# The first keys, the block scores and a table's layout around the input projection of a two-layer decoder trunk

## The reference, cut to what matters

```python
h = rmsnorm(x, a_norm);  proj = h @ w_in
qa, kc, vc, ksl, vsl, kwn, vwn, ga, qb, kb, vb, fb = split(proj)
qa = rope(rmsnorm(heads(qa)));  ksl, kwn = rope(rmsnorm(...))     # "first keys": ksl, kwn
k_cmp = rope(rmsnorm(gelu(blocks(kc) @ w1) @ w2));  v_cmp = ...    # 15 compressed blocks
p_c = masked_softmax(qa @ k_cmp);  o_c = p_c @ v_cmp               # "block scores"
o_s, o_w = selected and window branches                            # 256 keys: all of them
o_a = gates * (o_c, o_s, o_w)
qb, kb = rmsnorm(qb), rmsnorm(kb);  cum = cumsum(log_sigmoid(fb))
o_b = masked_softmax(qb @ kb + cum_q - cum_k) @ vb                 # fox heads
x = x + concat(o_a, o_b) @ w_out
```

## Time and profile before

| | before |
|---|---|
| runs | 1252.96, 1253.08, 1251.99 us (median 1252.96) |
| profiled execution, its own time | 1252.75 us |
| its span | 1250.9 us |
| PE busy | 1233.9 us, 99% of the span |
| PE weight loads / DVE / ACT / POOL busy | 82% / 79% / 65% / 3% |
| mean granted TensorE clock | 0.996 of full |

### The profile page before, as it was taken

One profiled execution on the slowest core, in us unless ns is written; L12 is line 12 of the kernel. 1 busy time (PEld: TensorE's weight loads), 2 busy tenths in 40 slices (PEclk: granted clock), 3 DMA queues, 4 the chain that ended last, 5 costly groups with the idle time before them and its releaser, 6 DMA issues.

```text
span 1250.9 us, 16182 instructions
## 1 busy us (share of the span) xinstructions
PE 1233.9 (99%) x6016; PEld 1021.7 (82%) x6021; DVE 982.4 (79%) x966; ACT 817.2 (65%) x891; POOL 36.5 (3%) x42
## 2 busy tenths in 40 slices
PE   8999999999999999999999999999999999999998
PEld 6789888888889886888888888888888888888886
DVE  5878664544567558999889889889889889889896
ACT  7555454343376547777777777777777777777774
POOL 1000000000000001000000000000000000000200
PEclk9899999999999999999999999999999999999999
DMA  9631135544444345999999999999999999999992
GB/s 356 253 135 35 53 150 202 202 179 172 169 184 143 131 152 201 361 392 373 398 365 375 398 365 371 398 372 368 395 355 368 408 381 368 387 369 364 396 420 92
DMA packets 53000, 361.36 MB, mean 289 GB/s; under 512 B 6048, under 2 KB 6560, under 8 KB 10944
## 3 DMA queue, kind: packets, MB, share of 16 engines
q1 hardware_dynamic: 49872, 349.34, 72.4%
q0 software_dynamic: 3056, 11.02, 2.2%
HBM read 354.56 MB, written 5.77 MB: 288 GB/s over the span
## 4 chain that ended last, share of the span: by engine, by line
PE 94%; DVE 2%; DMA 1%; SPq 1%; issue 1%; ACT 0%; DVEq 0%
PE bank L561 28%; PE bank L559 28%; PE bank L560 28%; PE bank L1099 2%; DMA raw<-in_weights 1%; PE bank L770 1%; PE bank L800 1%; PE bank L958 1%; PE bank L782 1%; PE bank L569 1%; PE bank L1064 0%; PE bank L669 0%; PE bank L846 0%; PE bank L716 0%; PE bank L1056 0%
## 5 line engine op out<-in xcount | busy, mean ns | idle before, releaser
L2150 DVE TENSOR_TENSOR low<-raw,whi 128x2048 fp32r<-128x2048 f32 x260 | 595.1, 2291 | 72.0 <-ACT whi L1497 70.8
L1497 ACT CAST whi<-raw 128x2048 fp32r<-128x2048 f32 x260 | 497.3, 1913 | 120.8 <-PE bank L561 119.8
L559 PE MATMUL bank<-whi,hT_hi 128*128 128x512 f32 (+1 forms) x1104 | 431.4, 391 | 1.7 <-DVE low L1646 1.1
L561 PE MATMUL bank<-whi,hT_lo 128*128 128x512 f32 (+1 forms) x1104 | 430.5, 390 | 0.0
L560 PE MATMUL bank<-low,hT_hi 128*128 128x512 f32 (+1 forms) x1104 | 429.8, 389 | 0.0
L559 PEld LDWEIGHTS bank<-whi,hT_hi 128*128 128x128 f32 x1104 | 208.1, 188 | 46.0 <-DVE hT_lo L1581 1.5
L560 PEld LDWEIGHTS bank<-low,hT_hi 128*128 128x128 f32 x1104 | 207.8, 188 | 43.8
L561 PEld LDWEIGHTS bank<-whi,hT_lo 128*128 128x128 f32 x1104 | 207.7, 188 | 43.1
L1563 DVE TENSOR_TENSOR low<-raw,whi 128x2048 fp32r<-128x2048 f32 x67 | 153.0, 2288 | 48.3 <-ACT whi L1190 48.2
L559 PE MATMUL bank<-whi,h_hi 128*128 128x512 f32 x440 | 183.1, 416 | 0.0
L561 PE MATMUL bank<-whi,h_lo 128*128 128x512 f32 x440 | 174.5, 397 | 0.0
(11 more groups left out here) (313 smaller groups left out, 823.6 us busy)
## 6 DMA issues: line engine op xcount, KB each, us to landing
raw<-in_weights SPq DMA_DIRECT2D x327, 1024.0 KB, 5.9
sums<-ybuf POOLq DMA_DIRECT2D x7, 512.0 KB, 6.9
arena<-in_compress SPq DMA_DIRECT2D x1, 1088.0 KB, 15.4
x<-in_x SPq DMA_DIRECT2D x2, 512.0 KB, 5.2
raw<-in_weights SPq DMA_DIRECT2D x4, 256.0 KB, 5.4
raw<-in_weights SPq DMA_DIRECT2D x2, 512.0 KB, 8.1
tokens<-hng POOLq DMA_DIRECT2D x2, 512.0 KB, 3.5
out<-x SPq DMA_DIRECT2D x4, 256.0 KB, 3.0
```

The costliest lines, as they stand in the source:

```text
L559: mm(out_, a_hi, b_hi, start=start, stop=False)
L561: return mm(out_, a_lo, b_hi, start=False, stop=stop)
L1497: nc.scalar.copy(whi[:, u % SPLIT, :, :], raw[:, u % RAW, :, :]).then_inc(S["w_hi"], 1)
L2150: V.tensor_tensor(low[:, u % RAW, :, :], raw[:, u % RAW, :, :], whi[:, u % SPLIT, :, :].bitcast(F32), ALU.subtract).then_inc(S["w_lo"], 1)
```

## The change

Four things: the table `sml` gets 124 more columns (426 to 550), with most entries at other places; on ACT the squares of group 0 come behind the copies of its result, and PE waits ahead of group 2 for the squares, since both use banks 4 and 5; on DVE `split(5)` moves behind the first keys; on PE `block_scores` moves from the middle of group 5 to its end.

```diff
-R_QN, R_KN, R_FQ, R_FK, R_ON, R_GB, R_FB, R_EPS = 0, 64, 128, 129, 130, 132, 156, 164
-R_NORM = 166
+R_QN, R_KN, R_FQ, R_FK, R_ON, R_GB, R_FB, R_EPS = 0, 64, 128, 129, 256, 258, 282, 130
+R_NORM = 290
@@ PE, in_group
                 if cg >= 2:
                     pe.wait_ge(S["proj"], 2 * (cg - 1))
+                if cg == 2:
+                    pe.wait_ge(S["squares"], 2)
@@ PE
-            in_group(5, {2: later_queries, 4: block_scores})
+            in_group(5, {2: later_queries})
+            block_scores()
             pe.wait_ge(S["head_done"], 4)
@@ ACT
-                if cg == 0:
-                    head_squares(0, 0, 256)
...
                 if cg == 0:
+                    head_squares(0, 0, 256)
                     head_root(0, 8)
@@ DVE
             head_sums(4, 0)
-            split(5)
...
             head_roots(4, 0)
             link(head_scale(keys, 4, 0, R_KN, keys))
             rope(keys, tab, 4, four(rA, 4), four(rB, 4)).then_inc(S["head_done"], 1)
+            split(5)
             dve.wait_ge(S["sw_hi"], 2)
```

## The result

| | before | after |
|---|---|---|
| median of the runs taken together | 1253.02 us (4 runs) | 1245.76 us (4 runs: 1246.83, 1245.91, 1245.61, 1245.12) |
| profiled execution, its own time; its span | 1252.75; 1250.9 | 1246.83; 1245.0 |
| PE busy | 1233.9 us | 1226.1 us |
| mean granted clock | 0.996 | 0.996 |

The ratio is 0.9944 with a 95% interval of 0.9927 to 0.9961: faster by 7.3 us (4.9 to 9.1). The forecast was 1253.6 us in 1250.4 to 1257.0. PE's busy time alone fell by 7.8 us, and around the input projection the new kernel has one more wait above 1 us than the old one (two for one).

A forecast was written before the change was run, and what follows sets the result against it. PE was taken as the bound, in the chain for 94% of 1250.9 us; -1.34 - 1.7 + 2.5 + 1.3 = +0.8 us on 1252.75 gave 1253.6 us, range 1250.4 to 1257.0.

The forecast's parts named there:

- The longer table: 124 more columns in `sml` shift the tiles declared behind it: 0, with bounds of -2 and +2 us.
- Rival four: The tiles' new places pay, up to 2 us or more off the sum: 1249.5 to 1251; chance 0.04.
- The wait and the keys: Input projection: DVE's keys ahead of split(5) remove PE's wait before the 64 small products, -1.34 us.
- PE's wait for the squares: Ahead of group 2: the new wait does not bind, 0 us, bounds 0 and 0.3 us.
- The clock at the first place: Near 45 us: 3.4 us at half clock in place of 6.7, -1.7 us, bounds -3.4 and 0.
- rival one: Behind group 5 the clock stays low into the attention: slower, 1255.3 or 1257.0 us; chance 0.25.
- The block scores: Behind group 5: without the second unit as cover, the chain through ACT and DVE delays PE, +2.5 us.
- the term of the clock: Behind group 5: 38 thin products make the clock fall again, +1.3 us, bounds 0 and +4.7.
- The table load on ACT: Before the exponential behind group 5: 1.28 us by the trace, without the 1.38 us drain of the skill's rule.
- The sum of the moves: Input projection and behind group 5 together: -1.34 - 1.7 + 2.5 + 1.3 = +0.8 us.
- the 459 GB/s: Rate assumed while the first units load: the table's 63 KB more take 0.14 us, counted as 0.

The follow-up runs named there:

- t_table: The kernel before with the longer table alone, no engine's order moved: 1244.83 us, ratio 0.9947.
- b_table_keys: The changed kernel with the block scores put back between the two units of group 5: 1241.44 us, ratio 0.9907.
- a_short_table: The changed kernel with the short table put back, so the three moves alone: 1254.20 us, ratio 1.0015.
- r_all128: The changed kernel with 128 bytes of pad ahead of the first tile, moving all tiles together: 1246.09 us, ratio 0.9951.
- t_pad224: The kernel before, old table, with the pad ahead of the attention's area 224 bytes wider: 1245.52 us, ratio 0.9945.
- t_pad480: The kernel before, old table, with the pad ahead of the attention's area 480 bytes wider: 1243.71 us, ratio 0.9922.
- p_rest_480: The kernel before with every tile from the attention's area on moved by 480 bytes except h2_hi and h2_lo: 1250.42 us, ratio 0.998.

## Why the prediction was wrong, point by point

- **The longer table** is the step that failed: "0 (rows 9: weight loads 188 ns each)", with bounds of 2 us. It measured -6.6 us (t_table), of the 7.3; less the clock, -8. The sum was right to ask about the new places and asked the wrong column. The length of a weight load is 188 ns in every kernel here, fast or slow. The pitch of the products was in the trace before: 233.5 ns between h products against 226.7 between most others. 6.8 ns x 1320 products is 9.0 us, and with that as the bound in place of 2 the range would have held the result. Rival four was the right mechanism, with its size set at a third and its chance at 0.04.
- **The wait and the keys**: -1.34 us forecast, and it is gone with 1.7 us of room (1.9 forecast). PE's wait for the squares never showed. By the square above the move is worth 3.3 to 5 us, more than the wait; by the estimate from the runs' clocks 0.4 to 1.2 of it is the wait and 2.0 to 2.8 is clock.
- **The clock at the first place**: -1.7 us, bounds -3.4 and 0. No fall in this execution, but none in t_table's either, where the wait still stands. In the mean of the runs the estimate gives -2.0 to -2.8, good to about 1 us: the forecast's size, though not by the forecast's mechanism of a shorter fall, as no profiled execution without the wait fell there at all. The runs agree with what the prediction quoted beside rival one from the Trainium skill (TensorE: Matmul & The Clock Gate, What's actually happening), that the moment of the change differs between runs. A single trace gives such a term no value, only bounds.
- **The block scores**: +2.5 us and +1.3 for the clock, 3.8 together. Measured +2.9 (beside the table alone) and +4.3 (beside table and keys). The chain came as written, with brackets of 1.65 and 1.57 us for 1.9 and 1.8. The prediction's T, the end of group 5's first unit, is here 82.46 - 5.45 = 77.0, so the L812 products start at T + 22.6. The sum had T + 19.7 at full clock, and T + 21.0 with its 1.3. But the clock was at 1.2 GHz for 6.9 us, which is 3.4 us of PE's work, all of it on the path: that gives T + 23.1, and the rest of the chain was 0.5 us shorter than worked out. That is a slip of the sum: T + 11.55 and one copy of 0.6 us are T + 12.2 and not T + 12.8. So the term of the clock was too small in this execution, by 2.1 us, though the clock was back by 91.9, before the point where rival one decides. Here too one execution is no measure: b_table_keys, where 38 thin products stand between the units, has a low stretch of like length, from about 80.4 to 87 us. Over the runs the scores' move costs 1.0 to 1.8 us of clock and 2.6 to 3.4 beside it. The prediction's T + 17.4 had 1.7 us of lost clock in it, so its own 3.8 us are 4.2 beside the clock and -0.4 of clock: the first too high, by the slip and up to 1 us more, the second too low. What rival one describes came once, in a_short_table's profiled execution: a further low stretch from 98.9 to 102.3 us.
- **The table load on ACT**, where rule and trace parted. The timeline of ACT in the changed kernel:

```profile
92.01 0.68 ACT L1265 ACTIVATE arena<-bank,sml 66x512 f32<-66x512 f32 x1 [0.17 <-PE bank L718]
92.71 1.28 ACT L1277 ACT_TABLE_LOAD   x1
94.00 0.42 ACT L1277 ACTIVATE arena<-arena 128x256 f32<-128x256 f32 x1
```

  The copy ends at 92.69, the load at 93.99, the exponential starts at 94.00. The load now lies on the path and costs its 1.28 us; the 1.38 more for a drain (the Trainium skill, ScalarE: Activation LUTs, What ACT_TABLE_LOAD costs) are not in this trace.
- **The sum of the moves**: +0.8 us forecast. Measured +1.9 (0.5 to 3.3) with the short table, and with the long one the whole change against the table alone, 0.9944 against 0.9947, no difference (less the clock, +2 in both pairs). The forecast lies between; without the table it would have stood.
- **Two readings**: the 459 GB/s are those of the row at 45 us, not of the time when the first units load, and the wait before 42.56 is 1.34 us, not 1.5. Neither changes the sum.

## What to carry to other kernels

Where PE's weight loads and its moving operand are both large and dense, try their tiles at the same remainder by 256 bytes, which paid here, and fix those places so that a small table declared earlier cannot shift them. Judge dense products by the distance from start to start, line by line: groups that run some ns slower than their like can show a place problem before any change is made. When small work is moved out from between two dense blocks, list what ACT and DVE did under the cover, and take big pieces that nobody waits for (here `split(14)`) out of that list first.

## What the runs showed of the hardware

A 128x512 product with a 128x128 load beside it starts every 226.7 ns when the loaded tile and the streamed one start at the same remainder by 256 bytes (in the changed kernel all `hT` products of the experts and the last products of each down projection), and mostly every 231 to 235 ns when they differ by 32, 64, 96 or 128, with no trace in the length of a load. That is 1.5 to 2% of the whole kernel where it hits all 4632 dense products (+19 us with `whi` off, +24 with `hT` and h2 off, of 1246). The absolute place does not matter (r_all128), and products behind slow ones, or behind the turns of `hact`, are slow too, for about six. That the period is 256 rests on t_pad224 and t_pad480, which lie 256 bytes apart and are alike; no wider distance was tried. Open: why there is such a rule (nothing here separates the load from the streaming read), why 96 bytes gave part of the gain, and which tile carries the 2.5 us of p_rest_480.
